# Alternating high and low weight products tile by tile in a two-block transformer kernel

## The reference, cut to what matters

```python
p = h @ w_l                                  # 2048 x 8704 or so, block 1
y_a = (attn * jax.nn.silu(z_a)) @ w_pa
y_b = (_fourier_mix(u_b) * jax.nn.silu(z_b)) @ w_pb
return (g_a * y_a + g_b * y_b) @ w_o
...
proj = u @ w_in[l].astype(f32)               # block 2
...
h = h + gate1 * (merged @ w_out[l].astype(f32))
ff = jax.nn.silu(u @ w_gate[l].astype(f32)) * (u @ w_up[l].astype(f32))
h = h + gate2 * (ff @ w_down[l].astype(f32))
```

## Time and profile before

| | |
|---|---|
| median of 3 runs | 2800.46 us (2799.1 to 2802.19) |
| the profiled execution | 2796.57 us, span 2794.7 us |
| granted TensorE clock, mean | 0.999 |
| TensorE products busy | 2759.4 us, 99% of the span |
| TensorE weight loads busy | 2384.1 us, 85% |
| VectorE busy | 2048.6 us, 73% |
| ScalarE busy | 1460.1 us, 52% |
| GpSimd busy | 379.5 us, 14% |
| transfers | 621.84 MB, mean 223 GB/s |

### The profile page before, as it was taken

The page is one execution under the profiler, slowest core; times in us unless marked ns, Lnnn a source line. Parts: engine busy times, 40 slices in busy tenths (PEclk is TensorE's granted clock), DMA queues, the critical chain, the costliest instruction groups (busy, mean ns, idle before and its releaser), DMA issues.

```text
span 2794.7 us, 42931 instructions
## 1 busy us (share of the span) xinstructions
PE 2759.4 (99%) x16354; PEld 2384.1 (85%) x16354; DVE 2048.6 (73%) x3589; ACT 1460.1 (52%) x2414; POOL 379.5 (14%) x958
## 2 busy tenths in 40 slices
PE   7999999999999999999999999999999999999999
PEld 4778888888888888888888888888888888888888
DVE  4468878888987788888888877778976555555554
ACT  3465544445566666666666444545454443344443
POOL 0014300000002344434343320000000000000000
PEclk9999999999999999999999999999999999999999
DMA  9946668888955455555555678888856555555564
GB/s 359 349 160 217 221 216 284 294 304 307 308 167 203 163 176 177 180 172 177 176 182 178 219 235 271 295 290 286 276 179 225 185 186 190 192 186 193 183 198 142
DMA packets 183582, 621.84 MB, mean 223 GB/s; under 512 B 20288, under 2 KB 28752, under 8 KB 182736
## 3 DMA queue, kind: packets, MB, share of 16 engines
q1 hardware_dynamic: 173360, 605.62, 63.8%
q10 hardware_dynamic: 10016, 13.47, 1.5%
HBM read 612.70 MB, written 4.21 MB: 221 GB/s over the span
## 4 chain that ended last, share of the span: by engine, by line
PE 82%; DVE 7%; ACT 4%; POOL 3%; DMA 2%; issue 2%; ACTq 0%; SPq 0%; DVEq 0%
PE ps L96 81%; DVE wlo L111 2%; POOL small L111 2%; DMA raw<-in_w 1%; POOL small L114 1%; DVE acc L117 1%; PE ps L99 1%; ACT whi L102 1%; DVE c_y L117 1%; ACT sb_l L102 1%; DMA raw<-in_w_s 0%; ACT L105 0%; DMA xc<-in_xc 0%; ACT sb_z L102 0%; DMA q_sw<-q_g 0%
## 5 line engine op out<-in xcount | busy, mean ns | idle before, releaser
L96 PE MATMUL ps<-act,whi 128*128 128x512 f32 (+1 forms) x6560 | 1657.8, 392 | 6.8 <-DVE p_x L111 5.8
L96 PEld LDWEIGHTS ps<-act,whi 128*128 128x128 f32 (+1 forms) x6560 | 1176.0, 188 | 224.0 <-issue 8.0
L111 DVE TENSOR_TENSOR wlo<-raw,whi 128x1024 fp32r<-128x1024 f32 (+3 forms) x883 | 1039.2, 1186 | 19.5 <-ACT whi L102 15.1
L102 ACT ACTIVATE whi<-raw 128x1024 fp32r<-128x1024 f32 (+3 forms) x883 | 897.1, 1028 | 260.2 <-PE ps L96 103.0
L96 PE MATMUL ps<-act,wlo 128*128 128x256 f32 (+2 forms) x6416 | 972.3, 290 | 0.0
L96 PEld LDWEIGHTS ps<-act,wlo 128*128 128x128 f32 (+1 forms) x6416 | 868.7, 190 | 56.2 <-issue 9.2
L117 DVE SCALAR_TENSOR_TENSOR acc<-raw,c_act,acc 128x1024 f32<-128x1024 f32 x210 | 268.3, 1278 | 0.0
L114 POOL TENSOR_SCALAR small<-small 128x2 f32<-128x2 f32 (+3 forms) x316 | 138.7, 439 | 950.1 <-DVE small L114 820.2
L111 POOL TENSOR_TENSOR small<-small 128x2 f32<-128x2 f32 (+1 forms) x460 | 166.5, 362 | 345.0 <-ACT u_u L102 310.8
L111 DVE TENSOR_TENSOR w_u<-w_u,ps 128x256 f32<-128x256 f32 x44 | 18.4, 421 | 99.3 <-ACT w_u L102 99.3
L111 DVE TENSOR_TENSOR w_g<-w_g,ps 128x256 f32<-128x256 f32 x44 | 18.4, 421 | 93.4 <-ACT w_g L102 93.4
(11 more groups left out here) (328 smaller groups left out, 2299.7 us busy)
## 6 DMA issues: line engine op xcount, KB each, us to landing
raw<-in_w SPq DMA_DIRECT2D x418, 512.0 KB, 4.7
raw<-in_w_mod SPq DMA_DIRECT2D x192, 512.0 KB, 5.3
raw<-in_w_gate SPq DMA_DIRECT2D x88, 512.0 KB, 4.4
raw<-in_w_up SPq DMA_DIRECT2D x88, 512.0 KB, 4.1
raw<-in_w_s SPq DMA_DIRECT2D x64, 512.0 KB, 6.9
raw<-in_w_out SPq DMA_DIRECT2D x64, 512.0 KB, 5.8
raw<-in_w_down SPq DMA_DIRECT2D x64, 448.0 KB, 4.4
raw<-in_w_ada SPq DMA_DIRECT2D x32, 512.0 KB, 5.0
```

The source lines that it names most:

```text
L96: return self.e.matmul(*args, **more)
L102: return self.e.activation(*args, **more)
L111: return self.e.tensor_tensor(*args)
```

## The change

The high and low products of one tile now follow each other directly. A new function `products(turn, tiles)` runs, for each tile, its high product, the wait for `lo`, the shift products where the tile is `late`, and its low product. A turn that isn't narrow runs the first half of its tiles in this way, then the side work, then the other half, whose last product signals `w_done`. The number of products, weight loads, transfers and operations of the other engines is the same, and the narrow turn is as before.

```diff
+        def products(turn, tiles):
+            n = 16 + turn.t
+            hi, lo = HI[n % NH], LO[n % NL]
+            for j in tiles:
+                u, kt = turn.tiles[j]
+                if kt == u.kts[0]:
+                    claim(u.bank)
+                b, w = PS[u.bank], slice(128 * j, 128 * j + 128)
+                if u.wide:
+                    mm(both(b[:, :]), hi[:, w], L[:, :, kt, :], kt == u.kts[0], False)
+                    mm(both(b[:, :]), hi[:, w], H[:, :, kt, :], False, False)
+                else:
+                    e.wait_ge(*on(u.rhs, kt))
+                    mm(both(b[:, :]), hi[:, w], X[u.rhs](kt), kt == u.kts[0], False)
+                e.wait_ge(*on("lo", n))
+                if u.late is not None:
...
+                if u.wide:
+                    p = mm(both(b[:, :]), lo[:, w], H[:, :, kt, :], False, kt == u.kts[-1])
+                else:
+                    p = mm(b[:, 256:512], lo[:, w], X[u.rhs](kt)[:, 0, :], False, kt == u.kts[-1])
+                if kt == u.kts[-1]:
+                    held[u.bank] = [("taken", u.name, u.i) if not u.wide else ("kv_v", u.i)]
+            return p
+
         for turn in TURNS:
...
-            for j, (u, kt) in enumerate(turn.tiles):
-                if turn.narrow:
-                    break
...
-                    mm(both(b[:, :]), w, X[u.rhs](kt), kt == u.kts[0], False)
+            split = 0 if turn.narrow else len(turn.tiles) // 2
+            if not turn.narrow:
+                products(turn, range(split))
...
-            if turn.narrow:
-                continue
-            e.wait_ge(*on("lo", n))
-            for j, (u, kt) in enumerate(turn.tiles):
...
-                    p = mm(b[:, 256:512], lo[:, w], X[u.rhs](kt)[:, 0, :], False, kt == u.kts[-1])
...
-            p.then_inc(*tell("pe_gemm", "w_done", n))
+            if not turn.narrow:
+                products(turn, range(split, len(turn.tiles))).then_inc(*tell("pe_gemm", "w_done", n))
```

More of the change, by code:

```diff
@@ L627, in pe @@
         held[4], held[5], held[6] = ([("kv_v", i)] for i in range(3))
+        def products(turn, tiles):
[14 more added lines that the diff above has]
+                if u.late is not None:
+                    name = "u" if u.rhs == "raw" else "u2"
+                    if kt == 0 and u.late == 0:
+                        claim(3)
+                        e.wait_ge(*on("shift", name))
+                    o = PS[3][:, 2 * u.late:2 * u.late + 2]
+                    mm(o, hi[:, w], SH[:, kt, :], kt == 0 and u.late == 0, False)
+                    p = mm(o, lo[:, w], SH[:, kt, :], False, kt == 15 and u.late == 1)
+                    if kt == 15 and u.late == 1:
+                        p.then_inc(*tell("pe_shift", "shift_sum", name))
+                        held[3] = [("offset", name)]
+                if u.wide:
[5 more added lines that the diff above has]
+            return p
         for turn in TURNS:
@@ L914, in pe @@
                 held[c] = [("g_ob", h)]
-            if turn.narrow:
-                continue
-            e.wait_ge(*on("lo", n))
-            for j, (u, kt) in enumerate(turn.tiles):
[L921 to L935, removed]
-                    p = mm(b[:, 256:512], lo[:, w], X[u.rhs](kt)[:, 0, :], False, kt == u.kts[-1])
-                if kt == u.kts[-1]:
-                    held[u.bank] = [("taken", u.name, u.i) if not u.wide else ("kv_v", u.i)]
-            p.then_inc(*tell("pe_gemm", "w_done", n))
+            if not turn.narrow:
+                products(turn, range(split, len(turn.tiles))).then_inc(*tell("pe_gemm", "w_done", n))
     def kv_end(u):
```

## The result

The changed kernel takes 2814.54 us (median, 2812.12 to 2818.49) against 2799.81 us of the kernel before: the ratio is 1.0053, with a 95% interval of 1.0041 to 1.0065. It is slower by half a per cent, and the forecast was 2814. The profiled execution took 2814.19 us, its span is 2812.4 us.

A forecast was written before the change was run, and what follows sets the result against it. TensorE, busy 2759.4 of 2794.7 us, was taken as the bound. Slower products (+12.0) and the earlier low weights (+1.4) on 2796.57 us gave 2810.0; 3.9 us to the runs' median made it 2814, range 2770 to 2840.

The forecast's parts named there:

- The pairs are slower: All turns of the usual form: a high and a low product of one tile cost 1.8 ns more, +12.0 us in sum.
- the high run behind the narrow turn: Trace row: eight high products after one full load beside a low product take 231 ns each, not 227.
- The size of a pair: High plus low product of one tile: 351.0 ns forecast against 349.2 before, bounds 340.3 and 355.
- the short turn: Turn of four tiles taken as nearest trace row: high products 232.5 ns, low ones 120 ns.
- The upper end: Worst cost of a tile's high and low product: 235 plus 120 ns, +5.8 ns each, +39 us.
- The prediction's own sign: In the new profile, a plain turn of 8 tiles takes 2.80 to 2.82 us if the forecast is right.
- a high record above 391 ns: In a plain turn of the new profile, the high products' mean record length exceeds 391 ns if the forecast is right.
- That all 6656 pairs pay: Every high and low product of one tile in the usual form pays 1.8 ns: 6656 x 1.8 = +12.0 us.
- The early need of the low weights: Merge stage, turn at 551.97: low weights needed 0.23 us after turn start, not 1.85; +1.4 us, between 0 and +2.4.
- The side work: Attention, transforms and delta rule start 1.40 us into the turn, not 1.85; taken as 0, between -2 and +5 us.
- A: Rival for the products' pace: it stays fast, 340.3 ns per high and low product, 2743 us; chance 0.13.
- C: Rival for the products' pace: extra time per product same in either order, only waits left, 2802 us; chance 0.18.

The follow-up runs named there:

- the kernel with twos: Changed kernel with two high products, then two low ones, and so on, the split around the side work kept; 2797.05 us against 2798.73 before.
- Three and one: Changed kernel with three high, three low, one high, one low product in each half turn; 2804.64 us against 2800.06 before.

## Why the prediction was right

The time came out at 2814.54 us where 2814 was forecast, with the sign and the mechanism. Not every step held: two terms were off in opposite directions, and that they came to half a microsecond of the forecast is luck.

*The pairs are slower.* Right, and the cause named, the full load beside each low product, is the larger part of it: narrowing that load to 64 columns brings a pair to 340 ns, and doing without 256-column products takes away the effect of the order. That the load beside the high product counts as well, about half as much, the prediction didn't see. The row that told it beforehand was the high run behind the narrow turn.

*The size of a pair.* Forecast 351.0 ns (+1.8), measured 353.7 in a plain turn (+4.5): too small by more than half. The step that failed is the choice of the short turn as the nearest case. It is a run of four, and groups of four do take 350 ns; a single pair is another pattern. The upper end, 355 ns, was the better guide. The high product has the difference: 232.5 ns was taken, with 235 as its upper end, and 2557.27 to 2557.51, 2557.63 to 2557.87 and 2557.98 to 2558.21 are 0.24, 0.24 and 0.23 us, on the mean 236.4. The low product was taken too high, 118.5 ns for 116.9. The prediction's own sign, a turn of 2.80 to 2.82 us, was missed with 2.83; the other, a high record above 391 ns, came true with 399. Its forecast range is also a little off in itself: 350 ns a pair and the wait give 2807 us, not 2804.

*That all 6656 pairs pay.* Wrong in the other direction. Over the 150 turns with side work between turns 250 and 400 the kernel lost nothing, and the kernel with pairs in side turns alone lost 2.2 us. The two errors cancel: +1.8 ns on every pair was +12.0 us; +33 ns a turn over the 392 turns from turn 475 on is 12.9 us. What the side turns show is a smaller loss, 1.5 ns a pair, and 2.7 us less idle time. Why a pair loses less there isn't shown. The first high product behind the side work is at the fast pace, but the kernel with side work behind the low run wins nothing from that.

*The early need of the low weights.* +1.4 us forecast, 1.1 us in two waits measured, the longer one (0.79 us) at 553.64, in the turn that was named. From that turn's first high to its first low product it is 1.18 us in place of 0.23, a delay of 0.95 us, the lag that the prediction read from the earlier trace rows. In the end it hardly costs: the kernel with twos needs the low weights early too and has no loss that can be told.

*The side work.* Taken at 0; the waits for the solve fell from 4.0 us in 4 waits to 1.9 in 1, the one for the attention stayed at 2.4. About -2 us, the lower end of its bounds.

*The rivals.* A (340 ns) is what a kernel with half the high weights does, so the pace itself was read rightly from the earlier trace rows. C, no change, also came out of the rule that the prediction drew on, that the next weights load while the present product runs. The Trainium skill, "TensorE: Matmul & The Clock Gate", "Part 2: What happens when you issue a matmul", also gives a load's time as its columns over 1.2 GHz; by that rule a column is 0.83 ns. The load records here agree in the step from width to width (187 ns for 128 columns, 161 for 96, 134 for 64 in the kernels with narrow high weights, 0.83 ns a column), but are some 80 ns longer than the rule's 107 ns for 128 columns. What the prediction concluded for this rival, that a covered load is free, isn't borne out: the load of 96 columns is over in time by the estimate above and costs 6 ns a pair more than one of 64.

## What to carry to other kernels

A busy TensorE can still have an inner pace. Read it from the distance between starts, once in each pattern of product and load that the trace offers, and price a new order by the row with the same pattern, not by the mean of its two sides.

An order that puts a short product beside a full weight load each time isn't better than runs of them; here all orders lie within 348 and 354 ns a pair, and the one that looked most natural was the slowest of those measured.

A term applied to all of a count should be checked against each stage of the program. Here the turns with side work, some 308 of 867, paid 2.2 of the 14.7 us.

## What the runs showed of the hardware that was not expected

- Weight loads that run beside a product still cost something when that product or its neighbour has 256 columns: 353.7, 346.3 and 340 ns a pair for high weights of 128, 96 and 64 columns. With the low weights at 64 columns and the high ones at 128 it is 347.5. When all products have 512 columns, full loads cost nothing (226.9 ns a product in either order).
- The pace isn't monotone in the length of the groups: 353.7 ns a pair for one, 348.8 for two, 350 for four, 349.2 for eight, 348.1 for sixteen. Three and one, with as many changes as two and two, takes 350.1 ns a pair in the feed-forward stage where two and two takes 348.4. Why a pattern settles at one pace or another stays open: no experiment here shows it.
